# Expert flags in TensorE's registers, waits where a bank is needed, and a one-group first scatter, in a mixture-of-experts layer

## What is computed

```python
logits = x @ router_w + router_b                    # 320 x 32
top_val, top_idx = lax.top_k(logits, 4)
gates = softmax(top_val)
for e in range(32):                                 # each expert on the tokens that chose it
    h = x[rows_of_e] @ w_up[e] + b_up[e]            # 1024 -> 2048
    glu, lin = minimum(h[:, :1024], 7), clip(h[:, 1024:], -7, 7)
    a = glu * sigmoid(1.702 * glu) * (lin + 1)
    y[rows_of_e] += gate_of_e * (a @ w_down[e] + b_down[e])
x = LN2(alpha * x + (1 + gate2) * y)
```

## Time and profile before

| | |
|---|---|
| median of three runs | 1500.77 us (1498.08 to 1501.68) |
| profiled execution, its time | 1503.88 us |
| its span, first to last instruction | 1501.8 us |
| TensorE busy | 1422.4 us, 95% of the span |
| VectorE, ScalarE busy | 496.6 us, 244.7 us |
| DMA, mean over the span | 349 GB/s, 523.72 MB |
| granted TensorE clock, mean | 0.968 |

### The profile page before, as it was taken

One profiled execution on the slowest core, in us unless ns is written; L12 is line 12 of the kernel. 1 busy time (PEld: TensorE's weight loads), 2 busy tenths in 40 slices (PEclk: granted clock), 3 DMA queues, 4 the chain that ended last, 5 costly groups with the idle time before them and its releaser, 6 DMA issues.

```text
span 1501.8 us, 22145 instructions
## 1 busy us (share of the span) xinstructions
PE 1422.4 (95%) x7677; PEld 579.9 (39%) x7678; DVE 496.6 (33%) x1128; ACT 244.7 (16%) x432; POOL 13.7 (1%) x22
## 2 busy tenths in 40 slices
PE   5999999999869999999999999999999999999993
PEld 2655656665433333333333323333333333333331
DVE  2111356554742223232223222323232322313336
ACT  0001334442101011111111111111111111101110
POOL 0000000000100000000000000000000000000000
PEclk9999999999859999999999999999999999999997
DMA  9949368997838699999999988999999999998941
GB/s 345 387 186 353 117 247 331 416 425 314 276 114 320 240 365 399 417 418 418 416 418 418 418 341 350 407 419 417 418 416 418 418 419 415 418 407 320 390 186 35
DMA packets 95716, 523.72 MB, mean 349 GB/s; under 512 B 10172, under 2 KB 10485, under 8 KB 55498
## 3 DMA queue, kind: packets, MB, share of 16 engines
q1 hardware_dynamic: 92512, 517.62, 86.1%
q0 software_dynamic: 1344, 4.90, 0.9%
q10 hardware_dynamic: 1834, 0.84, 0.3%
HBM read 519.87 MB, written 3.46 MB: 348 GB/s over the span
## 4 chain that ended last, share of the span: by engine, by line
PE 84%; DMA 8%; DVE 4%; SPq 2%; issue 2%; ACT 0%; DVEq 0%; ACTq 0%
PE ps L1646 29%; PE ps L1724 14%; PE ps L1589 7%; PE ps L1200 6%; PE ps L1263 5%; PE ps L1567 5%; DMA arena<-in_cache_v 4%; PE ps L1491 2%; PE ps L1638 2%; DMA arena<-in_w_in 2%; PE ps L1433 2%; PE ps L1260 2%; DMA arena<-in_w_up 2%; PE ps L1656 1%; PE ps L1235 1%
## 5 line engine op out<-in xcount | busy, mean ns | idle before, releaser
L1646 PE MATMUL ps<-arena 128*64 128x512 f32 x2048 | 457.9, 605 | 0.1
L1646 PEld LDWEIGHTS ps<-arena 128*64 128x64 f32 x2048 | 146.1, 139 | 311.3 <-issue 310.0
L1724 PE MATMUL ps<-arena 128*64 128x512 f32 x1024 | 226.8, 595 | 0.0
L1102 DVE TENSOR_TENSOR arena<-arena,ps 128x512 f32<-128x512 f32 (+1 forms) x198 | 124.4, 681 | 220.6 <-PE ps L1589 214.9
L1200 PE MATMUL ps<-arena 128*128 128x128 f32 (+4 forms) x1075 | 150.8, 281 | 28.1 <-DVE arena L728 10.2
L1146 DVE TENSOR_SCALAR arena<-ps 128x512 f32<-128x512 f32 (+1 forms) x35 | 24.2, 692 | 429.8 <-PE ps L1646 365.3
L1200 PEld LDWEIGHTS ps<-arena 128*128 128x128 f32 (+4 forms) x1075 | 115.7, 143 | 102.0 <-issue 80.5
L1724 PEld LDWEIGHTS ps<-arena 128*64 128x64 f32 x1024 | 70.7, 137 | 152.2 <-issue 152.2
L1589 PE MATMUL ps<-arena 64*128 64x512 f32 x444 | 122.1, 635 | 4.9 <-DVE arena L1126 4.6
L1567 PE MATMUL ps<-arena 128*64 128x512 f32 (+1 forms) x396 | 98.3, 615 | 2.3 <-DVE arena L1090 2.3
L673 ACT ACTIVATE arena<-arena 128x512 f32<-128x512 f32 (+1 forms) x35 | 22.1, 631 | 457.5 <-DVE arena L1146 457.5
(11 more groups left out here) (227 smaller groups left out, 836.6 us busy)
## 6 DMA issues: line engine op xcount, KB each, us to landing
arena<-in_w_up SPq DMA_DIRECT2D x256, 1024.0 KB, 13.9
arena<-in_w_down SPq DMA_DIRECT2D x128, 1024.0 KB, 11.9
arena<-in_w_ada SPq DMA_DIRECT2D x12, 2048.0 KB, 17.2
arena<-in_cache_k SPq DMA_DIRECT2D x16, 1536.0 KB, 14.3
arena<-in_cache_v SPq DMA_DIRECT2D x16, 1536.0 KB, 9.6
arena<-in_w_in SPq DMA_DIRECT2D x6, 2048.0 KB, 20.9
arena<-in_cache_k SPq DMA_DIRECT2D x32, 192.0 KB, 12.5
arena<-in_cache_v SPq DMA_DIRECT2D x32, 192.0 KB, 10.4
```

Of the source, the lines that this page charges most:

```text
L1102: ins = v_.tensor_tensor(acc[0:n, tt, 512 * h:512 * h + 512], acc[0:n, tt, 512 * h:512 * h + 512], bank(banks[h])[0:n], ALU.add)
L1646: ins = mm(bank(part)[64 * h:64 * h + 64], xe_t[:, 0, at:at + 64], up_w[:, k, FF * part + 512 * h:FF * part + 512 * h + 512], start=False, ...
L1724: ins = mm(bank(3)[64 * h:64 * h + 64], a_t[:, 0, at:at + 64], dn_w[:, kk, 512 * h:512 * h + 512], start=kk == 0, stop=kk == KC - 1)
```

## The change

On TensorE, the three value loads at the top of an item become one. The flags of the last and this item are kept in two registers (the first loaded ahead of the loop, the last one set to 0 there), the next item's flag is loaded behind `up`, and both registers are moved on at the end of an item. So item 0 scatters one group. The wait for the gates' copy leaves TensorE; ACT waits for its own copy and gives the first increments of `y_ready` and `selt_ready` behind it. The wait for both copies of gathered rows, behind `turn_gathered`, goes; VectorE copies the extra group first and counts it with a new semaphore, `extra_copied`, for which TensorE waits ahead of `down`; the transposes have the extra group first, too. `turn_act(1)`, with its wait, goes behind `add_up(1)`, and the wait for `at_ready[1]` goes from the head of `down` to its extra part.

```diff
@@ ACT, ahead of the loop
             act.wait_ge(route_ready, 1)
-            for counted_from_one in (y_ready, selt_ready):
-                act.sem_inc(counted_from_one, 1)
...
             nc.scalar.copy(gt_sb[0:NE, :], bank(6, 0, NTOK)[0:NE]).then_inc(gt_ready, 1)
+            act.wait_ge(gt_ready, 1)
+            for counted_from_one in (y_ready, selt_ready):
+                act.sem_inc(counted_from_one, 1)
@@ VectorE
             def gathered_turned(blocks, turn_no):
                 dve.wait_ge(gathered_turned_done, turn_no)
-                for v in range(blocks):
-                    w = 256 if v else 512
-                    ins = v_.tensor_copy(xe_t[:, v, 0:w], bank(1 + 2 * v, 0, w))
-                ins.then_inc(xe_ready, 1)
+                if blocks == 2:
+                    v_.tensor_copy(xe_t[:, 1, 0:256], bank(3, 0, 256)).then_inc(extra_copied, 1)
+                v_.tensor_copy(xe_t[:, 0, :], bank(1)).then_inc(xe_ready, 1)
...
                 with dve.Else():
+                    dve.sem_inc(extra_copied, 1)
                     gathered_turned(1, i + 2)
@@ TensorE
             def turn_gathered(blocks, turn_no):
                 pe.wait_ge(xn_ready, turn_no)
-                for v in range(blocks):
+                for v in reversed(range(blocks)):
...
             items = pe.value_load(flag_i[0:1, 0:1], min_val=NE, max_val=ITEMS)
+            last_reg, now_reg = pe.alloc_register("last_b"), pe.alloc_register("now_b")
+            pe.reg_mov(now_reg, pe.value_load(flag_i[0:1, 1:2], min_val=0, max_val=1))
+            pe.reg_mov(last_reg, 0)
             turn_gathered(2, 1)
             turn_gates()
-            pe.wait_ge(gt_ready, 1)
             with pe.Fori(0, items) as i:
-                now_b = pe.value_load(flag_i[0:1, bass.ds(i + 1, 1)], min_val=0, max_val=1)
-
-                last_b = pe.value_load(flag_i[0:1, bass.ds(i, 1)], min_val=0, max_val=ITEMS)
-                next_b = pe.value_load(flag_i[0:1, bass.ds(i + 2, 1)], min_val=0, max_val=1)
+                last_b, now_b = pe.snap(last_reg, min_val=0, max_val=1), pe.snap(now_reg, min_val=0, max_val=1)
...
+                next_b = pe.value_load(flag_i[0:1, bass.ds(i + 2, 1)], min_val=0, max_val=1)
                 pe.wait_ge(sel_ready, i + 2)
...
                 turn_act(0)
-                pe.wait_ge(a_ready[1], i + 1)
-                with pe.If(now_b > 0):
-                    turn_act(1)
-                with pe.Else():
-                    pe.sem_inc(at_done[1], 1)
                 with pe.If(next_b > 0):
                     turn_gathered(2, i + 2)
-                    pe.wait_ge(xe_ready, i + 2)
                 with pe.Else():
                     turn_gathered(1, i + 2)
                 with pe.If(last_b > 0):
                     add_up(1, 2)
                 with pe.Else():
                     add_up(1, 1)
+                pe.wait_ge(a_ready[1], i + 1)
+                with pe.If(now_b > 0):
+                    turn_act(1)
+                with pe.Else():
+                    pe.sem_inc(at_done[1], 1)
...
                     if blocks == 2:
+                        pe.wait_ge(at_ready[1], i + 1)
                         for m in ms:
...
+                pe.wait_ge(extra_copied, i + 2)
                 pe.wait_ge(at_ready[0], i + 1)
                 with pe.If(now_b > 0):
-                    pe.wait_ge(at_ready[1], i + 1)
                     down(2, (0, 1, 2, 3))
...
+                pe.reg_mov(last_reg, now_b)
+                pe.reg_mov(now_reg, next_b)
-            last_b = pe.value_load(flag_i[0:1, bass.ds(items, 1)], min_val=0, max_val=ITEMS)
+            last_b = pe.snap(last_reg, min_val=0, max_val=1)
```

More of the change, by code:

```diff
@@ L286, in layer_kernel @@
             sem, ("ga_done", "xn_ready", "gathered_turned_done", "xe_ready", "selt_done", "selt_ready", "sc_done", "sc_added"))
-        g2_done, y_done = sem("g2_done"), sem("y_done")
+        g2_done, y_done, extra_copied = sem("g2_done"), sem("y_done"), sem("extra_copied")
         ch_v, ch_end = sem("vector_chain"), sem("vector_chain_at_the_end")
```

## The result

The changed kernel takes 1485.75 us (median of 5, 1480.66 to 1488.48) against 1500.77 (median of 5): 15.0 us less, ratio 0.9899 with a 95% interval of 0.9877 to 0.9920. The forecast was 1484.8, range 1478.3 to 1492.5. A second set, taken later beside other kernels, gave 1486.27 (6 runs, ratio 0.9905, 0.9887 to 0.9922).

A forecast was written before the change was run, and what follows sets the result against it. TensorE was taken to bound the kernel, with DMA close behind. Direct terms of 14.4 us, less 0.8 given back, plus 2.4 for the clock against the median, made 16.0 off 1500.8: 1484.8 us, range 1478.3 to 1492.5.

The forecast's parts named there:

- Start of the loop: Entry of the expert loop: three value loads behind the wait for the gates' copy go, 2.3 us saved, bounds 1.0 to 3.1.
- First scatter: Item 0 scatters one group instead of two, over three token tiles: 2.6 us saved, with no cover seen under it.
- the wait for the copies in item 0: TensorE's wait for both copies of gathered rows, in item 0: its 1.4 us share of 4.3 for three places.
- The wait for the copies, the other two: The same wait ahead of the second and third double item: 2.9 us of the 4.3 forecast for three.
- The second activation: Double items: TensorE's 1.22 us wait for the second activation gets hidden behind moved transposes and a scatter, 3.1 us for three.
- Loads behind a double item: Gaps of about 0.71 us after each double item, laid to three value loads at the top, go: 2.1 us.
- The kept load: The one value load left, behind the up projection in all 32 items, fits the sequencer's lead and costs nothing.
- Given back: Part of the gains returns as TensorE's waits for weights from DMA: 0.8 us lost, bounds 0 to 2.
- Rival B: DMA becomes the bound, gains around the second and third double item turn into weight waits: 1492.7 us, chance 0.10.
- The clock: Four half-pace stretches, each following gaps, lose 8.3 us: half taken as saved, 4.2, less 0.6 for item 0, so 3.6.

## Why the prediction was right

The time was forecast within 1 us, but not every term. Against the profiled pair, in the order of the forecast:

- *Start of the loop, 2.3.* From the end of the last transposes to the first weight matmul 8.64 us before (437.96 to 446.60) and 6.15 after: 2.5. The size is right, the account incomplete. Before, the first block of the loop's code is fetched 4.3 us behind the transposes (442.25), since the loads stand behind the wait for the gates' copy; afterwards 1.9 us behind them (440.60), and in the kernel with the loads put back 2.4 (439.83 against 437.44). So the loads cost 2.2 us only in a row with that wait: without it they run beside the wait for VectorE's copy. The pause for the code itself stays, as the forecast's lower bound feared, 1.25 us before and 1.74 after. No run had the gates' wait put back alone.
- *First scatter, 2.6, and the wait for the copies in item 0, 1.4.* The step that failed: "I see no cover under it". Item 0 gained 1.5 from gather to down projection and 0.9 in its last scatter, 2.3 in place of 4.0, because the branch into the down projection waits for its block of code when reached for the first time, 2.1 us in this trace. With either edit undone it ran under the time that came back (0.0 for the wait, 1.4 for the scatters), and with the bodies exchanged it is gone. In the second trace of the changed kernel the 1.5 is 0.8.
- *The wait for the copies, the other two, 2.9.* 9.41 to 7.75, 1.66 each: 3.3. The 0.2 held back for branches was not needed.
- *The second activation, 3.1.* 1.41 each, 4.2. The forecast allowed 0.1 to 0.2 for ACT's copy and left out that the 64-row transposes start 0.2 us before the scatter ahead of them ends (885.03 against 884.07 + 1.13).
- *Loads behind a double item, 2.1.* The gaps 0.71, 0.69 and 0.71 are gone, 2.1, and come back with the loads. With them go 0.05 to 0.07 us ahead of each and 0.12 in the matmuls right behind it (from the first bias matmul to the first weight matmul 1.14 us in item 14 before, at the full clock, and 1.02 after): 2.7 in all.
- *The kept load, 0.* Right; four loads didn't touch a plain item whose weights were there, eight did.
- *Given back, 0.8.* Item 27 takes 1.1 us over its 32.38 in waits for weights, before 0.3 over 34.04 (32.38 and the wait of 1.66): 0.8. Rival B had its mechanism right and its size far too large. The HBM limit of 358 GB/s in the Trainium skill (DMA: Bandwidth & Descriptors, "Where 436 GB/s comes from") is worked out there as one core's half of what two share; this kernel runs on one core, and after the change it moves 418 GB/s from 900 to 1280 us.
- *The clock, 3.6.* From item 1 to item 29 the trace's record of the granted clock has 17.1 us at half pace before and 13.7 after, so 8.5 us lost and 6.8: 1.7. The two that followed the gap of 0.7 went; those at the heads of double items stayed. Over all profiled runs but the one left out: behind that gap 6 low stretches in 9 places (before, loads at top, the kernel before with the bias later), without it none in 27 (the others but that with eight loads). At heads with the bias ahead 18 in 30, with it twice 3 in 3, with the bias later none in 6. So the forecast's "each follows gaps" was true of one kind alone; the heads follow 2 us of bias matmuls. Of the Trainium skill's rule (TensorE: Matmul & The Clock Gate, "A second HAM failure mode"), by which all would go with the gaps, the runs bear out only the part for the gap of 0.7. The gaps of 1.2 and 1.6 us hardly mattered: with each of them put back alone, one head of three was low.
- The last transposes end 0.7 us later in this pair (438.68 against 437.96). That is spread and not the change: in the other traces they end at 436.0 in the kernel before and from 436.2 to 438.8 in the changed ones (442.2 in the one with eight loads).

Sum: 2.5 + 2.3 + 3.3 + 4.2 + 2.7 - 0.8 + 1.7 - 0.7 = 15.2, against 15.4 of span. The forecast in the profile's terms was 17.2, in the median's 16.0; measured 15.4 and 15.0. Item 0 and the clock were too high by 1.7 and 1.9, the other terms too low by 2.3. So that the time came within 1 us is in part luck: errors of both signs made it look better than its parts.

What the twelve runs leave open is how much the later bias gives. The medians say 7 us in the changed kernel and 2 in the kernel before, the ratio of the latter 1; the intervals are wide enough for 3 us in both. Both traces show clean heads. Why 2 us of bias matmuls bring the clock down at 18 heads and not at the other 12 stays open too.

## What to carry to other kernels

A value load costs its 0.73 us only where the sequencer has no lead over the array: look for it behind waits and behind runs of short instructions, and keep the sequencer's own rows beside the engine's. When a wait is removed at a place that the program reaches for the first time, look for code that was arriving under it, in the packets of the instruction queue; put the body that runs first directly behind its branch. When TensorE has a low stretch, list what stood ahead of it in many runs, idle time and one-row matmuls apart, before crediting its end to the gaps removed.

## What the runs showed of the hardware

- Code arrives in blocks: packets of 16 KB on the queue named instruction, four in item 0 and none in the 31 items behind it. TensorE's branch to such a place ends 1.34 to 1.42 us behind the packet's end, in twelve traces.
- A compare-and-branch takes 0.2 us in TensorE's sequencer (median), and once, on its first way into the down projection's second body, 1.7 to 2.8 us (1724, 1732, 1745, 1984, 2024, 2064, 2108, 2769 and 2784 ns in nine runs). With 1.5 to 1.6 us of waiting ahead of it, it took 0.42 to 0.65 (419, 447 and 647 ns), and 0.08 where it runs straight on. With the double body of the up projection made longer, the branch there took 3412 ns once.
- The sequencer's lead is 4.5 us behind an up projection of 64 matmuls and 2.2 to 2.6 us behind one that ends in 32-column matmuls; it goes where the weight loads wait for DMA.
- Sixteen or thirty-two one-row bias matmuls in a row (2 and 4 us) stood ahead of low stretches of 3.4 to 6.8 us at 18 of 30 heads and of 6.8 to 10.2 us at 3 of 3; with four weight slices ahead of them, there was none at 6.
- One execution in which TensorE took 106.5 us for each plain item in place of 29.4. Its trace holds no record of the granted clock, and the views print 1.00 for it. It came once, and no run tells why.
